# Interleaving the memory operand with the first projection of the second block, and spacing out the gating norm, in a two-block fp32 network kernel

## The reference

```python
def second_block(x, mem, ...):
    for l in range(DEPTH):                       # DEPTH = 2; the change is in l == 0
        h = rmsnorm_2(x, norm_mix[l])
        x = x + even_mixer(h, ...)               # l == 0
        x = x + mem_cross_attention(rmsnorm_2(x, norm_mem_q[l]), rmsnorm_2(mem, norm_mem_kv[l]), ...)
        x = x + swiglu(rmsnorm_2(x, norm_ffn[l]), ...)
    return x

def even_mixer(h, positions, w_in, q_gain, k_gain, w_s, b_s, ln_g, ln_b, w_out):
    q, k, v, pu, pv = split(h @ w_in)            # five parts of 512 columns
    q = partial_rope(rmsnorm_2(heads(q), q_gain), positions)
    k = partial_rope(rmsnorm_2(heads(k), k_gain), positions)
    a = moba_attention(q, k, heads(v))           # 8 heads of 64, causal over 256 tokens
    u, vg = gelu(pu), gelu(pv)
    g = u * (tril(w_s) @ layernorm(vg, ln_g, ln_b) + b_s)     # per group of 64, chunks of 128 tokens
    return concatenate([a, g]) @ w_out

def mem_cross_attention(h, mem_n, w_q, w_kv, ...):
    k, v = split(mem_n @ w_kv)                   # 256 memory tokens, 2048 columns
    ...
```

## Time and profile before

| | |
|---|---|
| time, median of 3 runs | 1671.75 us (1670.43 to 1680.97) |
| the profiled execution's own time | 1671.75 us |
| its span in the profile | 1669.9 us |
| mean granted TensorE clock | 0.979 of full speed |
| PE busy | 1582.2 us, 95% |
| DVE busy | 1122.8 us, 67% |
| ACT busy | 795.0 us, 48% |
| the stage from `ev_in` to `mix_out0` | about 802 to 933 us of the span |

### The profile page before, as it was taken

The page is one execution under the profiler, slowest core; times in us unless marked ns, Lnnn a source line. Parts: engine busy times, 40 slices in busy tenths (PEclk is TensorE's granted clock), DMA queues, the critical chain, the costliest instruction groups (busy, mean ns, idle before and its releaser), DMA issues.

```text
span 1669.9 us, 31425 instructions
## 1 busy us (share of the span) xinstructions
PE 1582.2 (95%) x12596; PEld 1516.0 (91%) x12596; DVE 1122.8 (67%) x2014; ACT 795.0 (48%) x1368; POOL 190.3 (11%) x200
## 2 busy tenths in 40 slices
PE   6988999999998999999999989999989899899997
PEld 5866898999997799999998879999979899799997
DVE  5884644767785758777868655766767566567666
ACT  4446234434453554444744555544445545554443
POOL 2680500100021020000100202000020001010000
PEclk9998797999999999999999999999999999999999
DMA  6411001454545135554534423655445354155652
GB/s 215 152 63 39 1 1 51 160 194 152 199 153 166 45 104 200 201 185 170 179 127 148 153 101 102 202 202 175 154 154 187 114 177 177 52 171 183 201 174 81
DMA packets 125813, 236.56 MB, mean 142 GB/s; under 512 B 2614, under 2 KB 50025, under 8 KB 125689
## 3 DMA queue, kind: packets, MB, share of 16 engines
q1 hardware_dynamic: 124393, 230.29, 39.8%
q0 software_dynamic: 1296, 4.53, 0.9%
HBM read 233.76 MB, written 1.05 MB: 141 GB/s over the span
## 4 chain that ended last, share of the span: by engine, by line
PE 84%; DVE 9%; ACT 3%; issue 3%; DMA 1%; SPq 0%; POOL 0%; DVEq 0%; ACTq 0%; POOLq 0%
PE ps L610 47%; PE ps L657 6%; PE ps L656 6%; PE ps L655 6%; PE ps L618 5%; DVE w_lo L2168 3%; PE ps L800 2%; PE ps L761 1%; PE ps L706 1%; PE ps L966 1%; PE ps L984 1%; DVE hidden L2219 1%; ACT w_hi L1561 1%; DVE mx L2514 1%; DVE u_lo L2188 1%
## 5 line engine op out<-in xcount | busy, mean ns | idle before, releaser
L1561 ACT ACTIVATE w_hi<-raw 128x1024 fp32r<-128x1024 f32 x440 | 460.9, 1051 | 295.2 <-PE ps L657 139.9
L2168 DVE TENSOR_TENSOR w_lo<-raw,w_hi 128x1024 fp32r<-128x1024 f32 x440 | 541.3, 1231 | 10.5 <-ACT w_hi L1561 10.4
L610 PE MATMUL ps<-u_hi,w_hi 128*128 128x256 f32 (+1 forms) x1480 | 428.8, 290 | 15.6 <-DVE u_lo L2188 5.2
L610 PE MATMUL ps<-u_hi,w_lo 128*128 128x256 f32 (+1 forms) x1480 | 421.9, 285 | 0.0
L610 PE MATMUL ps<-u_lo,w_hi 128*128 128x256 f32 (+1 forms) x1480 | 421.6, 285 | 0.0
L610 PEld LDWEIGHTS ps<-u_hi,w_hi 128*128 128x128 f32 x1480 | 281.6, 190 | 22.2 <-issue 7.1
L610 PEld LDWEIGHTS ps<-u_hi,w_lo 128*128 128x128 f32 x1480 | 281.9, 190 | 0.0
L610 PEld LDWEIGHTS ps<-u_lo,w_hi 128*128 128x128 f32 x1480 | 280.7, 190 | 0.6
L610 PE MATMUL ps<-a_hi,w_hi 128*128 128x256 f32 (+1 forms) x864 | 248.7, 288 | 6.7 <-DVE a_lo L2188 4.6
L610 PE MATMUL ps<-a_lo,w_hi 128*128 128x256 f32 (+1 forms) x864 | 245.4, 284 | 0.0
L610 PE MATMUL ps<-a_hi,w_lo 128*128 128x256 f32 (+1 forms) x864 | 245.1, 284 | 0.0
(11 more groups left out here) (414 smaller groups left out, 2315.2 us busy)
## 6 DMA issues: line engine op xcount, KB each, us to landing
raw<-in_w_ff_dram SPq DMA_DIRECT2D x32, 2048.0 KB, 8.7
raw<-in_ffn_w_gu_dram SPq DMA_DIRECT2D x44, 1024.0 KB, 7.3
raw<-in_ffn_w_down_dram SPq DMA_DIRECT2D x10, 2048.0 KB, 8.0
raw<-in_xa_w_kv_dram SPq DMA_DIRECT2D x8, 2048.0 KB, 9.2
raw<-in_od_w_in_dram SPq DMA_DIRECT2D x6, 2048.0 KB, 8.1
raw<-in_w_in_ab_dram SPq DMA_DIRECT2D x5, 2048.0 KB, 7.8
raw<-in_ev_w_in_dram SPq DMA_DIRECT2D x5, 2048.0 KB, 7.9
raw<-in_xa_w_q_dram SPq DMA_DIRECT2D x4, 2048.0 KB, 8.4
```

The lines of the kernel that those rows point to most:

```text
L610: mm = pe.matmul(bank[:, 0:n], wx[:, q, k * P:(k + 1) * P], x[ux][:, k, ts], start=k == 0 and i == 0, stop=k == KD - 1 and i == 2)
L1561: act.activation(quarter(w_hi, b, q), raw_quarter(b, q), ACT.Copy).then_inc(high_split, 1)
L2168: dve.tensor_tensor(quarter(w_lo, b, q), raw_quarter(b, q), quarter(w_hi, b, q).bitcast(F32), ALU.subtract)\
```

## The change

It has three parts.

1. The memory operand is no longer made ahead of the norm's scale. On both engines two chunks of it follow each of the four steps t of `ev_in` block 0: on ACT `gelu(0, t)`, `split_high(b+1, t)`, two chunks; on DVE `project_ev(0, t)`, `split_low(b+1, t-1)`, two chunks. DVE's split of quarter 3 of block 0, which stood ahead of the wait for the scale, now stands behind `project_ev(0, 0)`.
2. On ACT gelu now stands ahead of the split in each step; for block 1 `stream` does that.
3. In the pair stage the pieces of the gating norm that were in the steps 2, 3, 4, 5 of DVE are now in 3, 5, 6, 7 (ACT's logarithm and exponential from step 3 to 4), and the last tile of `xkv0`, a split of quarter 2 of `mix_out0` block 1 and `pair_result(7)` stand in a ninth step ahead of the gating products.

```diff
@@ ACT
-                if layer == 0:
-                    memory_operand()
                 norm_rs(rs[:, REAL], SEQ)
...
-                    for i in range(2):
-                        for t in range(4):
-                            split_high(phases["ev_in"].first + i + 1, t)
-                            gelu(i, t)
+                    for t in range(4):
+                        gelu(0, t)
+                        split_high(phases["ev_in"].first + 1, t)
+                        memory_operand([2 * t, 2 * t + 1])
+                    stream("ev_in", gelu, 1, 1)
...
-                        if k == 3:
+                        if k == 4:
                             act.wait_ge(M["g_stat"], 2)
@@ DVE
             for layer in range(2):
+                rms_ready()
+
                 def memory_low(chunks=range(KD)):
...
-                if layer == 0:
-                    memory_low()
-                    split_low(phases["ev_in"].first, 3)
-                rms_ready()
...
                     for t in range(4):
                         project_ev(0, t, tile_at[b] + t)
-                        if t >= 1:
-                            split_low(b + 1, t - 1)
+                        split_low(b + 1, t - 1)
+                        memory_low([2 * t, 2 * t + 1])
...
-                        if k == 2:
+                        if k == 3:
                             dve.wait_ge(M["g_sq"], 1)
...
-                        if k == 3:
+                        if k == 5:
                             dve.wait_ge(M["g_ln"], 1)
...
-                        if k == 4:
+                        if k == 6:
                             link(dve.tensor_tensor(gv, gv, ln_g.unsqueeze(1).to_broadcast([P, 2, BLOCK]), ALU.mult))
-                        if k == 5:
+                        if k == 7:
                             dve.tensor_tensor(gv, gv, ln_b.unsqueeze(1).to_broadcast([P, 2, BLOCK]), ALU.add)\
                                 .then_inc(M["g_n"], 1)
 
-                    for k in range(8):
+                    for k in range(9):
                         if k >= 1:
                             memory_tiles(2 * k - 1, 2 * k)
-                        pair_maximum(k)
-                        pair_normalise(k)
-                        memory_tiles(2 * k, 2 * k + 1)
+                        if k < 8:
+                            pair_maximum(k)
+                            pair_normalise(k)
+                            memory_tiles(2 * k, 2 * k + 1)
                         if k >= 1:
                             pair_result(k - 1)
-                        gate_norm(k)
-                    b = phases["xkv0"].first + 3
-                    project_memory(3, 3, tile_at[b] + 3)
+                        if k < 8:
+                            gate_norm(k)
                     for c in range(2):
                         dve.wait_ge(M["g_mixed"], c + 1)
                         ...
-                    pair_result(7)
                     for c in range(2):
                         ...
                         low_part(product[1][:, 4:8, ts], g_out(c), product[0][:, 4:8, ts])
-                    split_low(b + 1, 2)
```

## The result

The changed kernel takes 1683.36 us in the median of 16 runs (1678.19 to 1690.65), the kernel before 1673.38 us (1667.86 to 1681.98, 16 runs). The ratio is 1.0052, 95% interval 1.0035 to 1.0069: 8.7 us slower (5.9 to 11.5). The direction was forecast, and that the change stays within 1%; the size was forecast as 5.8 us, and 1683.36 lies outside the range that ended at 1681.5.

The account below looks back on a forecast made before the run. The prediction took PE, busy 95% of the span, to bound the whole kernel. Memory chunks +4.1 and the pair stage's end +1.7 made +5.8 us on 1671.75: forecast 1677.6 us, range 1672.5 to 1681.5.

Parts of the forecast that it names:

- Part 1, +4.1: Memory chunks in pairs in `ev_in` block 0: ACT and DVE take turns, token block 1 ends 4.1 us later.
- the first wait: PE at the first token tile of `ev_in` block 1 waits 3.6 us for the split of quarter 1.
- The second wait of 0.5: PE waits 0.5 us for the split of quarter 3, before the next two token tiles of `ev_in` block 1.
- Part 3, +1.7: End of the pair stage: the gating norm's late last piece delays the gating products, PE goes on 1.7 us later.
- The wait of 0.2 us that was to go: Pair stage, step 4: the norm's piece on DVE stood before a split PE waited 0.2 us for; that wait goes.
- So it stays: Behind `ev_in` token block 1: no later wait of PE swallows the delay, so the +4.1 us remains.
- The clock: Rival: PE's granted clock falls in the new pauses in `ev_in` and the pair stage's end; 1679 to 1681 us, chance 0.17.
- both fall: Clock losses behind `ev_in`'s new wait (+0.9 net) and at the pair stage's end (+1.4): 1679.9 us; clock rival's chance 0.17.
- a clock below 1.00 near 816 or 935 us: Sign of being wrong: granted clock well below 1.00 at `ev_in` block 1 or the pair stage's end.
- the new waits are each shorter than that one: Argument against a clock fall: PE's new waits are shorter than its longest, 4.3 us, behind which the clock was 0.79.
- Only one term: Rival: only the pair stage's end costs (1673.5 us) or only the `ev_in` memory chunks (1675.9 us); chance 0.14.
- faster: Rival: PE's waits of 0.2, 1.3 and 1.1 us in `ev_in` and the pair stage go; 1669.1 us, chance 0.06.

Follow-up runs that it names:

- the pause filled: Part 1 of the change on the kernel before, plus 28 matmuls with unread results in PE's pause behind norm_turn; ratio 1.0037 to the kernel before.

## Why the prediction was right and wrong

*Part 1, +4.1.* Right in mechanism and size for a PE at full clock. Rounds were 3.88 and 3.05 us, and the first wait 3.6. (The pieces of the first round add up to 3.85, not the 3.88 that the forecast wrote and the trace shows; that agreement is luck by 0.03 us.) The second wait of 0.5 is there only with the pause filled, as 0.42 us; the tiles take 0.7 us longer with it, which is why A is +4.31 and not +4.1. In the changed kernel itself the fallen clock takes its place.

*Part 3, +1.7.* Right in size, +1.79 and +1.80 at clock 1.00, and in the working, which put all four product operations behind `pair_result(7)`. What the working does not tell apart, and what I took wrongly before the experiments, is the cause: not the norm's late piece alone, the ninth step alone costs 0.95 of it. The split was covered, as I wrote, the gap that it fills was not free. The wait of 0.2 us that was to go came back one step later as 0.4.

*"So it stays."* Right: B is the same to 0.06 us in every kernel where it can be told from A.

*The clock.* This is the step that failed. The prediction had it as a rival at 0.17, "both fall", and left it out of the sum, that is at nothing, though its own last paragraph names a clock below 1.00 near 816 or 935 us as a sign of being wrong. Behind the pause of 3.6 us the clock fell in four of four profiles, and behind the others of 2.8 us and more (2.8, 3.3, 3.8) too. The four token tiles took 1.3 us longer by it three times and 2.4 once. Net of the second wait, which it hides, this cost 0.6 us three times and 1.7 once; I had said 0.9. Behind the 2.4 us in front of the gating it fell in two of five profiles, for 0.3 us. So the sum should have been about 7 to 8, not 5.8: the sections of the two profiles give +7.0 and +7.85. The argument against the rival, "the new waits are each shorter than that one" of 4.3 us, was no argument: one of 2.8 us was enough. The rule of the Trainium skill (TensorE: Matmul & The Clock Gate, Why this matters for your kernels), that idle gaps between bursts of matmuls bring the lower clock, agrees with the filled pause: 1.00 there, 0.50 to 0.72 behind the open one.

*The base and the range.* The clock alone does not carry the time out of the range: 1671.75 plus the sections' 7.0 to 7.85 is 1678.8 to 1679.6. The sum was made against one execution of 1671.75 us, the median of three. The 107 timed executions of that kernel have a mean of 1675.1 (standard error 0.4) and its four sets have the medians 1673.4, 1673.5, 1675.8 and 1673.6. The changed kernel has 1683.3 (0.8) over 26. The difference of the means is 8.2 (0.9), or 8.8 (1.0) against the 49 executions of the kernel before that were taken beside it: above the sections, by less than two standard errors. The forecast by median moves to 1679.2 with the base of 1673.38, and to 1680.4 to 1681.2 with the sections' 7.0 to 7.85; the last 2 to 3 us to 1683.36 I can put down only to the scatter of medians over so wide a spread, which is not shown. A range that carries both had to end near 1685.

*The rivals.* "Only one term" and "faster" fell with the sections A and C, both positive.

*Where the scatter comes from* I did not test. The profiles show it ahead of the stage: the x27 tile begins between 799.7 and 803.6 us in ten profiles and between 807.9 and 810.2 in four (the changed kernel's first is one), with a granted clock of 0.66 to 0.71 between 168 and 200 us where the ten have 0.75 to 0.81, in code that all of them share. Why an execution takes the one or the other is open.

## What to carry to other kernels

Work that one engine does "in pairs between the steps" joins the path as soon as each piece waits for another engine that itself waits for the steps: add up one round of evacuation, function, split, chunk and handoffs before moving anything out of a covered place. Price a new wait of the tensor engine at more than its length: if it is of the size that brought a fall every time here (2.8 us and more), count the slow matmuls behind it in the sum, not among the rivals, and then see whether the next wait gives them back. And take the base of a forecast from several executions where the times scatter more than the effect; judge the effect by stage lengths between marks in the chain, which here agreed to 0.06 us where the times scattered by 16.

## What was not expected of the hardware

The same wait can cost differently in each execution. The 1.9 us wait for L2188 (L2186, L2187 or L2192 in the others) ahead of the x27 tile is in all fourteen profiles; behind it the tile took 3.44 to 3.47 us in six of them and 4.92 to 4.99 in eight. In this stage waits of 2.8 us and more were followed by a fall in seven of seven, waits of 1.1 to 1.3 in none of nine, and those of 1.9 to 2.4 only sometimes. The rest of the same profiles agrees: the wait in front of L800 near 88 us, 2.8 or 4.3 us long, has a fall beside it in all fourteen, and the one of 2.6 us for L2760 (L2758, L2759 or L2764 in others) near 520 us in eleven. And the mean granted clock of an execution goes with its time: fitted over the timed runs, each kernel about its own mean, 0.001 of it goes with 1.2 us.
